# A hybrid decoder block on one core: the recurrent projection as seven half-block products, the convolution reordered, warm-up and filler matmuls

## The reference

```python
h = rms_norm(x, norm_mix_g[l])
proj = h @ w_in[l]                      # (256, 7168): xr, gr, q, k, v, two gates
xr, gr = proj[..., o0:o1], proj[..., o1:o2]
xc = conv_general_dilated(xr, conv_w, padding=[(3, 0)], feature_group_count=1024) + conv_b
r = sigmoid(einsum('bsnc,ncd->bsnd', xb, w_a) + b_a)      # xb: xc in 16 blocks of 64 channels
i = sigmoid(einsum('bsnc,ncd->bsnd', xb, w_x) + b_x)
# a scan over time with exp(-8 r softplus(-lambda)), then times gelu(gr)
```

## Time and profile before

| | us |
|---|---|
| median of 3 runs | 1210.28 (1209.37 to 1212.29) |
| profiled execution, its own time | 1208.98 |
| its span | 1207.2 |
| mean granted clock of TensorE | 0.992 |

### The profile page before, as it was taken

One profiled execution on the slowest core, in us unless ns is written; L12 is line 12 of the kernel. 1 busy time (PEld: TensorE's weight loads), 2 busy tenths in 40 slices (PEclk: granted clock), 3 DMA queues, 4 the chain that ended last, 5 costly groups with the idle time before them and its releaser, 6 DMA issues.

```text
span 1207.2 us, 15141 instructions
## 1 busy us (share of the span) xinstructions
PE 1152.7 (95%) x6206; PEld 591.4 (49%) x6206; DVE 358.6 (30%) x672; ACT 175.4 (15%) x350; POOL 30.6 (3%) x29
## 2 busy tenths in 40 slices
PE   9999999999999999999999989989898989898997
PEld 7589999986343433434343333333333333342433
DVE  2956778973412121111212020211111111111111
ACT  3160343103110110101010000001010101010102
POOL 1000000080000000000000000000000000000000
PEclk9999999999999999999999999999999999999999
DMA  9595417489999999999999999999999999999997
GB/s 284 190 293 177 146 63 279 158 311 368 414 422 428 426 438 422 435 427 434 427 433 427 438 423 437 428 433 428 433 429 432 432 431 428 432 429 429 428 425 290
DMA packets 52913, 452.96 MB, mean 375 GB/s; under 512 B 7668, under 2 KB 8814, under 8 KB 34318
## 3 DMA queue, kind: packets, MB, share of 16 engines
q1 hardware_dynamic: 52878, 452.47, 90.9%
HBM read 450.35 MB, written 1.06 MB: 374 GB/s over the span
## 4 chain that ended last, share of the span: by engine, by line
PE 68%; DMA 29%; DVE 1%; issue 0%; SPq 0%; ACT 0%; DVEq 0%; ACTq 0%
PE bank L1940 27%; DMA arena<-in_w_up_e 16%; PE bank L1748 11%; PE banks L1940 9%; DMA arena<-in_w_gate_e 8%; DMA w_gate_sb<-in_w_gate_e 5%; PE bank L1629 3%; PE banks L1889 3%; PE bank L1837 2%; PE banks L1748 1%; PE bank L1646 1%; PE banks L1663 1%; PE bank L1983 1%; PE bank L1663 1%; PE banks L2102 1%; PE banks L2161 1%
## 5 line engine op out<-in xcount | busy, mean ns | idle before, releaser
L1940 PE MATMUL bank<-arena 128*64 128x512 f32 x1032 | 238.6, 607 | 20.9 <-DMA arena<-in_w_gate_e 13.3
L1940 PEld LDWEIGHTS bank<-arena 128*64 128x64 f32 x1032 | 72.4, 139 | 162.6 <-issue 147.8
L1940 PE MATMUL bank<-w_gate_sb,arena 128*64 128x512 f32 x508 | 117.7, 611 | 9.7 <-DMA w_gate_sb<-in_w_gate_e 9.6
L1940 PE MATMUL bank<-w_up_sb,arena 128*64 128x512 f32 x508 | 112.4, 594 | 12.2 <-DMA w_up_sb<-in_w_up_e 12.2
L1940 PE MATMUL bank<-w_down_sb,arena 128*64 128x512 f32 x480 | 105.5, 592 | 0.0
L1515 DVE TENSOR_SCALAR arena<-bank 128x512 f32<-128x512 f32 x32 | 22.1, 691 | 257.9 <-PE bank L1940 256.9
L1426 DVE TENSOR_TENSOR arena<-banks,g2T 128x512 f32<-128x512 f32 (+1 forms) x32 | 21.9, 683 | 200.6 <-PE banks L1889 199.8
L1523 DVE TENSOR_SCALAR arena<-bank 128x512 f32<-128x512 f32 x32 | 22.1, 691 | 189.8 <-PE bank L1940 189.8
L1940 PEld LDWEIGHTS bank<-w_up_sb,arena 128*64 128x64 f32 x508 | 35.6, 137 | 83.6 <-issue 65.2
L1940 PEld LDWEIGHTS bank<-w_gate_sb,arena 128*64 128x64 f32 x508 | 35.3, 140 | 82.4 <-issue 68.6
L1940 PEld LDWEIGHTS bank<-w_down_sb,arena 128*64 128x64 f32 x480 | 34.5, 137 | 65.7 <-issue 64.6
(11 more groups left out here) (371 smaller groups left out, 1175.4 us busy)
## 6 DMA issues: line engine op xcount, KB each, us to landing
w_down_sb<-in_w_down_e SPq DMA_DIRECT2D x30, 2048.0 KB, 34.5
arena<-in_w_up_e SPq DMA_DIRECT2D x13, 4096.0 KB, 39.3
arena<-in_w_gate_e SPq DMA_DIRECT2D x13, 4096.0 KB, 30.8
w_up_sb<-in_w_up_e SPq DMA_DIRECT2D x12, 4096.0 KB, 37.6
w_gate_sb<-in_w_gate_e SPq DMA_DIRECT2D x12, 4096.0 KB, 30.0
arena<-in_w_down_e SPq DMA_DIRECT2D x14, 2048.0 KB, 29.3
w_gate_sb<-in_w_down_e SPq DMA_DIRECT2D x14, 2048.0 KB, 29.3
w_gate_sb<-in_w_gate_e SPq DMA_DIRECT2D x7, 2048.0 KB, 13.9
```

The source lines that it names most:

```text
L1940: ins = eng.matmul(ps[b * JB:(b + 1) * JB, :], lhsT, w[:, h * CH:(h + 1) * CH], **flags)
```

## The change

The recurrent projection is split like the other blocks: weights in four blocks of 512 x 512 (`xr_blocks`: 11, 12, 21, 22, loaded in this order, 1 MB each), tokens in two halves and the contraction in two. TensorE forms seven products (`xr_product`) in the order 0, 2, 4, 1, 3, 6, 5; product 0 needs the first token half alone and stands ahead of the transposes of the second. VectorE forms three more weight sums and one in place of a block (`xr_12`, `xr_two`, `xr_11`, `xr_21`), the token sums earlier, and five adds of parts (`xr_part`). The units of `xr` on ScalarE become two copies. Since channels are now complete in quarters, the convolution goes over channel pairs 4-5, 6-7, 0-1, 2-3, and the gates and swaps follow. Softplus and lambda work on VectorE moves behind the value's adds, and its lambda exponentials on ScalarE behind the decay exponentials. The value weights have places of their own (`value_low`) and are issued without a wait for the units; the q chunk is issued after the projection. GpSimd clears the bias rows after the value products instead of at the start. TensorE's warm-up reads a tile that VectorE sets, and has 11 matmuls instead of 10 and two more behind the gain's transpose; two pairs of bf16 filler matmuls stand in the routing. The sums are float32 and change rounding alone.

```diff
-WARM = 10
+WARM = 11
+XR_ORDER = (0, 2, 4, 1, 3, 6, 5)
+CONV_ORDER = (2, 3, 0, 1)
@@ sync
-            for t in range(TT):
-                eng.dma_start(hn[:, t, :], A["x"][0, t * P:(t + 1) * P, :]).then_inc(x_loaded[t], 16)
+            eng.dma_start(hn[:, 0, :], A["x"][0, 0:P, :]).then_inc(x_loaded[0], 16)
             eng.dma_start(gain[:, :], ...)
+            eng.dma_start(hn[:, 1, :], A["x"][0, P:T, :]).then_inc(x_loaded[1], 16)
+            for b in range(4):
+                rows, col = b // 2 * CH, COLUMN["xr"] + b % 2 * CH
+                eng.dma_start(xr_blocks[b], A["w_in"][0][rows:rows + CH, col:col + CH].rearrange("(k p) n -> p k n", p=P)
+                              ).then_inc(xr_loaded[b], 16)
-            chunk(0)
...
-            chunk(1)
...
+            eng.wait_ge(chunk_loaded[0], 16)
+            chunk(2)
             eng.wait_ge(chunk_loaded[1], 16)
             eng.dma_start(value_high, ...)
-            chunk(2)
...
+            eng.wait_ge(s["unit_done"], xr_done(5))
+            eng.wait_ge(chunk_loaded[0], 32)
+            chunk(4)
             eng.wait_ge(s["conv_ready"], 2)
-            swap_halves(0, 4, s["gate_inputs_loaded"])
+            swap_halves(4, 8, s["gate_inputs_loaded"])
@@ gpsimd
-            eng.wait_ge(s["constants_ready"], 5)
+            eng.wait_ge(s["unit_done"], unit("v", 7) + 1)
             eng.memset(brow, 0.0).then_inc(s["bias_rows_cleared"], 1)
@@ scalar
+                if t == 1:
+                    eng.wait_ge(s["unit_done"], xr_done(0))
+                    eng.activation(xr_quarters[2], quarters(xr_bank[0]), ACT.Copy).then_inc(s["unit_out"], 1)
...
+            eng.wait_ge(s["unit_done"], xr_done(2))
+            eng.activation(xr_quarters[0], quarters(xr_bank[2]), ACT.Copy).then_inc(s["unit_out"], 6)
...
+            eng.wait_ge(s["lambda_sums_ready"], 2)
+            eng.activation(lam[:, 2:4], lam[:, 0:2], ACT.Exp).then_inc(s["lambda_exps_ready"], 1)
             unit_out(unit("q"))
@@ vector
+            eng.memset(wT[:, 0:P], 1.0).then_inc(s["warm_tile_ready"], 1)
...
+            norm_high(0)
+            eng.wait_ge(xr_loaded[0], 16)
+            eng.wait_ge(xr_loaded[1], 16)
+            eng.tensor_tensor(xr_12, xr_12, xr_11, ALU.subtract).then_inc(s["sums_ready"], 1)
+            norm_high(1)
...
+            eng.tensor_tensor(xr_two, xr_22, xr_12, ALU.subtract).then_inc(s["sums_ready"], 1)
...
+            eng.tensor_tensor(xr_11, xr_two, xr_11, ALU.subtract).then_inc(s["sums_ready"], 1)
...
+            eng.tensor_tensor(xr_21, xr_21, xr_two, ALU.subtract).then_inc(s["sums_ready"], 1)
...
+            xr_part(1, xr_q12, xr_q21, 0)
+            xr_part(4, xr_q22, xr_q12, 1)
...
+            low, high = value_low, value_high
+            xr_part(3, xr_q22, xr_q22, 2)
+            xr_part(3, xr_q21, xr_q12, 1)
+            eng.wait_ge(chunk_loaded[0], 32)
+            eng.wait_ge(chunk_loaded[1], 32)
+            eng.tensor_tensor(weight_sums[0], high[:, 0:KQ], low[:, 0:KQ], ALU.subtract).then_inc(s["sums_ready"], 1)
+            xr_part(6, xr_q12, xr_q12, 4)
+            for n in range(4):
+                if n == 1:
+                    xr_part(5, xr_q21, xr_q21, 5)
+                if n == 2:
+                    eng.wait_ge(s["sums_ready"], SUMS_OF_XR + 1)
+                    eng.tensor_tensor(weight_sums[1], high[:, KQ:KC], weight_sums[0], ALU.subtract).then_inc(s["sums_ready"], 1)
+                    eng.wait_ge(s["unit_out"], 7)
+                if n == 3:
+                    eng.wait_ge(s["unit_done"], xr_done(6))
+                    eng.wait_ge(s["sums_ready"], SUMS_OF_XR + 2)
+                    eng.tensor_tensor(weight_sums[3], low[:, KQ:KC], weight_sums[1], ALU.subtract).then_inc(s["sums_ready"], 1)
+                eng.wait_ge(s["parts_ready"], 5 if n < 2 else 6)
+                for c in (2 * CONV_ORDER[n], 2 * CONV_ORDER[n] + 1):
...
+                ins.then_inc(s["conv_ready"], 1)
+            eng.tensor_tensor(weight_sums[2], high[:, KQ:KC], high[:, 0:KQ], ALU.subtract).then_inc(s["sums_ready"], 1)
@@ tensor
+            eng.wait_ge(s["warm_tile_ready"], 1)
+            warm(WARM)
...
+            warm(2)
...
+            turn(hn, 0, [s["x_normed"]] * 2, s["norm_turned"])
+            xr_product(0)
+            turn(hn, 1, [s["x_normed"]] * 2, s["norm_turned"])
+            for n in (2, 4, 1):
+                xr_product(n)
...
+            for n in (3, 6, 5):
+                xr_product(n)
...
+            eng.wait_ge(s["sums_ready"], SUMS_OF_XR + 4)
+            eng.wait_ge(s["parts_ready"], 5)
             value_product(token_sums[2], weight_sums[2], bank[1], 2)
...
             eng.matmul(slot_place[1], ones[:, 0:P], r_mask[:, 0, :], start=True, stop=False)
+            keep_busy()
             eng.wait_ge(s["mask_ready"], 2)
             eng.matmul(slot_place[1], tri, r_mask[:, 1, :], start=False, stop=True).then_inc(s["slots_done"], 1)
+            keep_busy()
```

More of the change, by code:

```diff
@@ L83, in unit, with xr_done @@
     return [i for i, (m, _, _) in enumerate(UNITS) if m == name][n]
-def units_through(i):
-    return max(u for u, (m, c, _) in enumerate(UNITS) if (m, c) == STREAM[i]) + 1
+def xr_done(n):
+    return XR_ORDER.index(n) + 1
 def block_done(j, n):
@@ L1025, in _, with norm_high @@
             eng.wait_ge(s["rows_ready"], 1)
-            for t in range(TT):
+            def norm_high(t):
                 eng.wait_ge(s["norm_turned"], 2 * t + 2)
@@ L1042, in _, with tap @@
             link(eng.tensor_scalar(sp[:, 6, :], lruT, -1.0, 0.0, ALU.mult, ALU.max))
+            low, high = value_low, value_high
[18 more added lines that the diff above has]
+                for c in (2 * CONV_ORDER[n], 2 * CONV_ORDER[n] + 1):
+                    def tap(w):
+                        return pvT[:, V_CONVW + w * KC + c:V_CONVW + w * KC + c + 1]
+                    link(eng.tensor_scalar(xcT[:, c, :], xrT[:, c, :], tap(3), pvT[:, V_CONVB + c:V_CONVB + c + 1],
+                                           ALU.mult, ALU.add))
+                    for back in (1, 2, 3):
+                        ins = eng.scalar_tensor_tensor(out=xcT[:, c, back:], in0=xrT[:, c, 0:T - back],
+                                                       scalar=tap(3 - back), in1=xcT[:, c, back:],
+                                                       op0=ALU.mult, op1=ALU.add)
+                        if back < 3 or c % 2 == 0:
+                            link(ins)
+                ins.then_inc(s["conv_ready"], 1)
@@ L1592, in _, with warm @@
         def _(eng):
+            def warm(count):
+                for _ in range(count):
+                    eng.matmul(bank[6][:, 0:P], wT[:, 0:P], wT[:, 0:P], start=True, stop=True)
+            eng.wait_ge(s["warm_tile_ready"], 1)
+            warm(WARM)
             eng.wait_ge(s["identity_ready"], 2)
-            for _ in range(WARM):
-                eng.matmul(bank[6][:, 0:P], ident[:, :], ident[:, :], start=True, stop=True)
             eng.wait_ge(s["gain_then_block_21_loaded"], 16)
             eng.transpose(bank[7][:, 0:KC], gain[:, :], ident[0:KC, 0:KC]).then_inc(s["rows_turned"], 1)
+            warm(2)
             def turn(src, t, ready, turned):
@@ L1657, in _ @@
                        ).then_inc(s["bias_vector_done"], 1)
-            for n in range(2, 4):
-                product(unit("xr") + n, rhs=hT)
+            for n in (3, 6, 5):
+                xr_product(n)
             def value_product(lhsT, w, ps, count=1):
@@ L1664, in value_product @@
                 ins.then_inc(s["unit_done"], count)
-            first, second, low, high = hT[:, :, 0:P], hT[:, :, P:T], wst[:, 0], value_high
+            first, second, low, high = hT[:, :, 0:P], hT[:, :, P:T], value_low, value_high
             eng.wait_ge(chunk_loaded[0], 32)
@@ L1898, in gather_two, with keep_busy @@
                 return ins
+            def keep_busy():
+                for _ in range(2):
+                    eng.matmul(bank[0][:, :], ones[:, 0:JB].bitcast(BF16), ones[:, :].bitcast(BF16), start=True, stop=True)
             out_product(0)
```

213 lines of the change are left out of this document (100 added, 113 removed).

## The result

The changed kernel takes 1213.78 us in the median of 12 runs (1213.26 to 1217.76), the kernel before 1210.24 us (1209.37 to 1212.57, 12 runs): a ratio of 1.003, 95% interval 1.0021 to 1.0038. That is a loss of 3.5 us, and it lies on the 0.3% that the prediction took as the least that a measurement tells from no change.

What follows compares the result with a forecast made beforehand. TensorE sets the pace from 93.9 to 503 us, expert weights to 1117 us, so early delays reach the end. 1208.98 + 2.5 (VectorE's late sum) + 1.7 (lower clock) = 1213.2 us; range 1207.5 to 1217.

Steps and rivals of the forecast that it cites:

- the sum: Whole kernel: 1208.98 us profiled before, plus 2.5 us stall and 1.7 us lower clock, gives 1213.2 us; chance 0.40.
- VectorE's term: VectorE's weight sums, adds and convolution take 25.8 us from the value weights' landing, making the seventh value product 2.5 us later.
- Value weights: Both 2 MB loads land at 35.7 us, bounds 34.8 to 36.5; earlier issue behind the same tables gains nothing.
- Rival (b): Value weights land by 32.0 us, TensorE stays last, gates start at 61.2 us: 1207.7 us; chance 0.14.
- Projection: Seven TensorE products of 3.57 us from 9.6 to 37.2 us; 3.1 us gained, but off the path.
- The clock: TensorE's clock falls after the new 2.6 us idle stretch, costing 1.7 us; likelihood 6 in 10.
- A first product at half clock: The projection's first product would take 3.6 us more, still within the slack of the seventh value product.
- Lambda: VectorE waits 4.9 us for the moved lambda exponentials, hidden by 5.3 us of idle time with 0.5 to 1 us spare.
- Fillers: Two pairs of matmuls in routing waits cost 0 to 0.3 us together and bring nothing; taken at 0.
- signs: Seventh value product starts at 61 to 62 us after 2 to 3 us idle, gates at 65 to 66.6 us.

Runs made afterwards that it cites:

- run 1: Changed kernel with the seven small loads of gate blocks, router, its bias and the norm's gain issued behind the two value-weight loads: 1210.65 us, ratio 0.9998 to the kernel before.
- run 6: Changed kernel with VectorE's last value-weight sum formed twice, one subtraction more on its chain: 1217.9 us, ratio 1.0055 to the kernel before.
- run 7: Changed kernel with the sum of product 6 and the convolution of channels 4 and 5 moved ahead of VectorE's wait for value weights: 1211.83 us, ratio 1.0002.
- run 4: Changed kernel without the two pairs of filler matmuls in the routing: 1216.15 us, ratio 1.0039 to the kernel before.
- run 5: Changed kernel measured again, unedited: 1215.25 us, ratio 1.0029 to the kernel before.
- run 8: First measurement of early blocks, made from the changed kernel: 1208.99 us, ratio 0.9982 to the kernel before.
- run 3: Changed kernel with three and nine small matmuls filling TensorE's waits ahead of the last two value products: 1213.53 us, ratio 1.0021 to the kernel before.
- run 9: Kernel before with the two pairs of routing filler matmuls added, nothing else: 1210.1 us, ratio 0.9995 to the kernel before.
- early blocks: Changed kernel reordered: tables behind value weights, projection blocks loaded in reading order, first half of rows finished before the second is squared: 1208.99 us, again 1210.15 us.
- run 10: The early blocks kernel without the two pairs of routing filler matmuls: 1209.44 us, ratio 0.9986 to the kernel before.
- run 2: Kernel before with its small table loads likewise issued behind the value weights: 1210.14 us, ratio 1.0001 to the unedited kernel before.
- run 12: Second measurement of early blocks, unedited: 1210.15 us, ratio 0.9992 to the kernel before.
- run 11: The early blocks kernel with the kernel before's shorter warm-up of 10 matmuls on the identity: 1210.52 us, ratio 0.9995 to the kernel before.

## Why the prediction was right, and where it was not

The outcome, +3.5 us on the 0.3% between "same" and "slower", is near the +4.2 us forecast, and the mechanism is the one forecast. That the number came so near is in part luck (see the sum). Step by step:

- **VectorE's term.** 25.8 us from the landing to weight sum 2. Measured 62.35 - 36.52 = 25.8 us; weight sum 3 after 19.7 (19.8 forecast), idle 2.39 us ahead of V6 (2.6). Runs 1, 6 and 7 show it as the cause: earlier landing, longer chain, another order.
- **Value weights.** Forecast 35.7 us, bounds 34.8 to 36.5; measured 36.5 us here, and up to 38.3 us in other executions. Mis-sized by 0.8 us: 4 MB in one piece at the 376 GB/s of the earlier trace rows were taken, and in the changed kernel the rate was lower (339 GB/s). The landing lay at the upper bound here, and beyond it in runs 4, 5 and 6 (37.1, 36.7 and 38.3 us). The forecast that an earlier place in the list gains nothing behind the same tables held: the loads left at 21.82 and 22.30 us. These windows answer to those of the earlier trace rows:

```profile
22.00:24.00 2.00, 2.00 (x21) 2.00 (x20) 2.00 (x2) 0.00 (x0) 0.00 (x0) 1.00 0.55 93
24.00:36.00 12.00, 12.00 (x104) 11.23 (x103) 6.02 (x10) 0.21 (x1) 0.00 (x0) 1.00 0.91 339
```

- **Rival (b).** Its condition was that the weights land by 32.0 us. Run 1 met it nearly (32.7 us) and TensorE was last, as stated. Its price of -1.3 us did not come: the gates started at 62.12 instead of 61.2 us, since the projection ended 0.6 us later than forecast and VectorE's last sum, done at 58.4 us, was level with TensorE, and the median was 0.1 us over the kernel before. Its argument against, that the tables must drain in any order, holds only where they stand ahead, and the change leaves them there.
- **Projection.** Forecast end 37.2 us, measured 37.9 us. P0 started at 9.97 instead of 9.6 us. I had taken only the block's landing for its wait. The timeline names ScalarE, which waited until 7.32 us for the second half of x and squared it before it wrote the first transposes out (done at 9.92 us); but the block landed at about the same time, 7.9 us behind its issue at 2.07 us, so either alone would have held P0. The wait for the third block, 0.70 us, ended at 15.39 us (15.0 forecast). Both vanish in TensorE's slack, as forecast; run 8 shows what they are worth without it.
- **The clock.** Price 1.7 us: measured 5.40 - 3.70 = 1.7 us. The chance of 6 in 10 stands beside three of four profiles and 10 of 12 low mean clocks (run 3). A first product at half clock was put at 3.6 us more; in runs 4 to 7 it took 1.6 us more (granted clock 0.69 over the product in run 5, so the lower level held for a part of it).
- **Lambda.** VectorE (its timeline below) waited 5.12 us for ScalarE where 4.9 us were forecast, and of the cover of 5.33 us 1.66 us were left: hidden.

```profile
79.64 0.16 DVE L1160 TENSOR_TENSOR lam<-lam 128x1 f32<-128x1 f32 x1 [5.12 <-ACT lam L829]
...
91.02 2.29 DVE L1179 TENSOR_TENSOR arena<-w_down_sb,w_gate_sb 128x2048 f32<-128x2048 f32 x1 [1.66 <-DMA w_down_sb<-in_w_in]
```

- **Fillers, the step whose reason failed.** "They bring nothing here: the granted clock is 1.00 in the windows on both sides." One execution with the full clock says nothing of the others. Of the 102 runs of the kernel before that stand beside these kernels, 34 lie above 1211.5 us; with the fillers added none of 11 did (run 9). The cost of nothing was right, the benefit was mis-sized by up to 0.8 us. That is not resolved on a median, and on early blocks (run 10) the median did not rise without them.
- **The sum.** It met the median because its errors cancel. It started from 1208.98 us, which is 1.3 us under the median of before and under each of the 12 runs beside it (1209.37 at the lowest). In the profiled execution of after the shift at the gates was 5.2 us, not 4.2: 0.8 us of later landing and 0.2 us of handovers. V6 at 62.35 and the gates at 67.67 us lie outside the 61 to 62 and 65 to 66.6 us named as signs. Over many executions the lower clock comes in only a part of them (one profile of four without it: -0.4 us), and the fillers give back up to 0.8 us (run 9). As an estimate from these, 1210.24 + 5.2 - 0.4 - 0.8 is 1214.2 us, against 1213.78 measured.

## What to carry to other kernels

When products are saved at the price of sums on another engine, lay out that engine's list from its last input's landing to its last output, and compare its end with TensorE's; here a saving of 3 us turned into a loss of 3.5 us by a sum that waited for loads, which landed 4 us later than they could, behind small tables. Moving those tables undid it. Work whose inputs are there belongs ahead of a wait, not behind it (run 7). And a granted clock read in one profiled execution is one draw: whether a filler or a warm-up is worth its place is seen in the spread of many runs.

## What the hardware showed that was not expected

- **The clock can fall behind waits of 0.50 and 0.71 us.** In run 4 that was so after the routing, where TensorE did only small matmuls around them; in the kernel before and in runs 2 and 10 the same waits were followed by the full clock.
- **P0 ran at either clock.** With the longer warm-up, waits of 0.18, 1.36, 1.51, 1.76, 1.78 and 2.09 us (runs 8, 12, 10, 3, 1 and the changed kernel) were followed by P0 in 3.8 us, waits of 2.20, 2.27, 2.73 and 2.76 us (runs 5, 4, 6, 7) by 5.4 to 5.5 us; with the shorter one 1.59 us was followed by 5.47 us (run 11). These are one execution each, and whether the wait or the work ahead of it decides was not tried.
- **The first megabyte lands at different times.** With the same loads ahead of it, it landed 7.9 us behind its issue in the changed kernel, 8.0 in run 5 and 8.5 us in run 6, and P0 started at 9.97, 10.07 and 10.58 us; in the two profiles of early blocks it took 6.2 and 7.7 us, and P0 started at 8.40 and 9.45 us. That is up to 1.5 us for one and the same list of instructions, and V6 of runs 8 and 12 is apart by 1.55 us. What makes it land later was not tried.
